# Low halves of three weight blocks made by ScalarE and an adding transfer, in place of a VectorE subtraction

## The chip, the cores and the metric

One program on one core of a Trainium2 chip. The metric is the device time of one execution in microseconds. Before the change the median of three executions is 1394.92 us.

## The reference

Two blocks of a transformer follow each other on 512 tokens of width 1024: a gated MLP layer with a spatial mix, a dilated attention layer, then a second block with two kinds of attention and a feed-forward part. The change lies in that last feed-forward part alone:

```python
D_FF = ((8 * D_MODEL // 3 + 255) // 256) * 256        # 2816
h2 = _modulate(x, ln2_g[l], sh2, sc2)
y = (jax.nn.silu(h2 @ w_gate[l]) * (h2 @ w_up[l])) @ w_down[l]
x = x + g2[:, None, :] * y
```

All arrays are float32.

## The kernel before

**Precision.** Each operand of a matmul is kept as two tiles: a high half, which is the value rounded to float32r by a ScalarE copy, and a low half, the value minus the high half, made by a VectorE subtraction. A product is then three matmuls: high by high, high by low, low by high.

**The feed-forward part.** The 2816 hidden columns are 22 chunks of 128. `FF_GROUPS` cuts them into three groups of 8, 8 and 6 chunks. The first four chunks of group 0 are "whole" (plain matmuls), and the other 18 are "fast" chunks: 4 in group 0, 8 in group 1, 6 in group 2. After each group four "down" chunks multiply by `w_down`.

**A fast chunk.** The gate and up weights of a chunk are cut into four blocks of 128x512 that lie side by side in one raw tile `w_raw` (1 MB, 128x2048). A scheme of Strassen's kind computes the chunk with seven products of 12 matmuls (128x256) each. Their weights are seven blocks: B11, B22 and B21 are blocks of the raw tile as they stand (`PLAIN`), while P1, T3, T2 and T4 are sums, made on VectorE by `two_sums`, `three_sum` and `four_sum`. For each of the seven, `part_round` (ScalarE, L1103) writes the high half into a slot of `w_hi` and `part_rest` (VectorE, L1977) the low half into a slot of `w_lo`.

**Order on TensorE.** For chunk i: product 1 (B11) of i, product 3 (B22) and 4 (T4) of i-1, then product 6 (T2), 5 (P1), 2 (B21), 7 (T3) of i. Each slot of `w_hi` and `w_lo` exists once, so the halves for chunk i+1 are written after the product of chunk i that used the slot.

**Order on ScalarE.** For chunk i: the copy of product 1's result out of PSUM (`half_1`, L1108), B11 of i+1, B22 of i, a silu of i-1, T4 of i, `half_2` (L1113), T2 of i+1, the high half of the gated result of i-1, `half_5`, P1 and B21 of i+1, another silu, `half_3`, T3 of i+1. Product 6 waits for `half_1`, product 7 for `half_2`, product 3 for `half_5`, product 4 for `half_3`. Every engine runs its list in order.

**Raw tiles.** There are two `w_raw` tiles, used in turn. SyncE's queue holds the loads, one for each chunk (`tail_load`, L597). The load for a row waits until the row two before it has been read: for a fast chunk that is VectorE's low half of B22.

GpSimd has nothing to do in this part of the kernel. The profile's line numbers are those of the code before; in the changed kernel L1103 is L1123, L1977 is L1999, and so on.

Of the kernel before, what the change touches and what calls it, by code (L numbers as in the profile page):

```python
# [21 lines left out]
F32 = mybir.dt.float32  # L22
F32R = mybir.dt.float32r
ACT = mybir.ActivationFunctionType
# [73 lines left out]


PRODUCT_AT, PART_AT = product_counts(), part_counts()  # L100

# [48 lines left out]
def program(nc, d):  # L152
# [181 lines left out]
    def sem(name):  # L334
        return nc.alloc_semaphore(name)
# [43 lines left out]
    part_made, part_hi_done, part_lo_done, product_done = sem("part_made"), sem("part_hi_done"), sem("part_lo_done"), sem("product_done")  # L379
    half_1_out, half_2_out, half_3_out, half_5_out = sem("half_1_out"), sem("half_2_out"), sem("half_3_out"), sem("half_5_out")  # L380
    gate_first_done, up_first_done, up_second_done = sem("gate_first_done"), sem("up_first_done"), sem("up_second_done")
    silu_first, silu_second = sem("silu_first"), sem("silu_second")


# [29 lines left out]
    def slot_of(tiles, j):  # L414

        return tiles[j // 4][:, TOK * (j % 4):TOK * (j % 4) + TOK]
# [44 lines left out]
    with block:  # L461
# [3 lines left out]
        def _(sp):  # L465
# [122 lines left out]
            def tail_load(n):  # L588

                used = FF_GROUPS[2][1] * 256 if n >= ROW_OF["whole", W_DOWN[2]] else 2048  # L590
                src = weights[bass.ds(n, 1), :, 0:used].rearrange("a p n -> p (a n)")
                kind, before = ROWS[n - 2]
                if kind == "whole":
                    sp.wait_ge(lo_done, before - 1)
                else:
                    sp.wait_ge(part_lo_done, PART_AT[before, B22])
                sp.dma_start(w_raw[n % 2][:, 0:used], src).then_inc(w_loaded[n % 2], 16)  # L597

            for n in range(W_GU1 + 6, W_END):
# [8 lines left out]
        @block.gpsimd  # L608
        def _(pool):
            def stage(j, par):  # L610

                ge(pool, mix_done, j - 1)
                nc.gpsimd.tensor_tensor(v_stage[par][:, :, :], v[:, :, bass.ds(j * P, P)],
                                        v_stat[:, 5, :].unsqueeze(2).broadcast_to([P, TB, P]), ALU.mult).then_inc(v_staged, 1)

            def sum_squares(k, total, tile):

                for m in range(1, KT - 1):
                    pool.wait_ge(sq_ready, 8 * k + m + 1)
                    if m > 1:  # L620
                        pool.wait_ge(sq_added, 6 * k + m - 1)
                    nc.gpsimd.tensor_tensor(total, tile(0) if m == 1 else total, tile(m), ALU.add).then_inc(sq_added, 1)

            nc.gpsimd.memset(one_row[:, :], 1.0).then_inc(one_ready, 1)
            nc.gpsimd.memset(idle[:, :].bitcast(F32), 0.0).then_inc(idle_ready, 1)
            nc.gpsimd.memset(half_r[:, :].bitcast(F32), 0.0).then_inc(half_zeroed, 1)
            nc.gpsimd.memset(eps_tile[:, :], EPS)
            nc.gpsimd.memset(ones_r[:, :].bitcast(F32), 1.0).then_inc(ones_ready, 1)
            pool.wait_ge(half_zeroed, 1)
            pool.wait_ge(ones_ready, 1)  # L630
            for e in range(2):
                if e:
                    pool.wait_ge(half_ready, 1)
                part = slice(64 * e, 64 * e + 64)
                nc.gpsimd.memset(half_r[part, part].bitcast(F32), 1.0).then_inc(half_ready, 1)
            pool.wait_ge(half_ready, 2)
            pool.wait_ge(v_stat_dve, 3)
            stage(0, 0)
            stage(1, 1)
            with pool.Fori(1, AT // 2) as i:  # L640
                for par in range(2):
                    stage(2 * i + par, par)

            sum_squares(1, sq_sum[:, :], lambda m: sq_a[m % 2][:, :])

            def quarters(m):

                pool.wait_ge(exp_done, 4 * m + 4)
                ge(pool, spread_done, m)
                stats = row_stat[:, 0, :, :].rearrange("p k n -> p (k n)").unsqueeze(1).broadcast_to([P, 4, 16])  # L650
                nc.gpsimd.tensor_tensor(row_apart[:, :, :], stats, own_quarter.unsqueeze(2).broadcast_to([P, 4, 16]), ALU.mult).then_inc(apart_done, 1)

            pool.wait_ge(blocks_loaded, 16)
            for m in range(QH):
                quarters(m)
            pool.wait_ge(pv_done, 4 * QH)
            nc.gpsimd.memset(wf_hi[:, :, :].bitcast(F32), 0.0).then_inc(wf_zeroed, 1)
            nc.gpsimd.memset(wf_lo[:, :, :].bitcast(F32), 0.0).then_inc(wf_zeroed, 1)
            sum_squares(2, sq_sum[:, :], lambda m: sq[m % 2][:, :])
            sum_squares(3, sq_sum[:, :], lambda m: sq[m % 2][:, :])  # L660


        @block.scalar
        def _(act):
# [427 lines left out]
            def part_round(i, j):  # L1092

                group, f, n = FAST[i]
                if j in PLAIN:
                    act.wait_ge(w_loaded[n % 2], 16 * (n // 2))
                else:
                    act.wait_ge(part_made, 3 * i + {P1: 1, T3: 1, T2: 2, T4: 3}[j])
                if i == FAST_OF[group][0]:
                    act.wait_ge(mm_done, 2 * W_DOWN[group] - (2 if j < 4 else 0))  # L1100
                else:
                    act.wait_ge(product_done, PRODUCT_AT[i - 1, USED_BY[j]])
                nc.scalar.activation(slot_of(w_hi, j), part_full(i, j), ACT.Copy).then_inc(part_hi_done, 1)  # L1103

            def half_1_copy(i):
                act.wait_ge(product_done, PRODUCT_AT[i, 1])
# [79 lines left out]
        def _(dve):  # L1186
# [764 lines left out]
            def two_sums(i):  # L1951

                n = FAST[i][2]
                dve.wait_ge(w_loaded[n % 2], 16 * (n // 2))
                if i > 0:
                    dve.wait_ge(part_lo_done, PART_AT[i - 1, T3])
                pairs = w_raw[n % 2][:, 0:3 * TOK].rearrange("p (b n) -> p b n", b=3)
                nc.vector.tensor_tensor(part_sums[:, :, :], pairs[:, 0:2, :], pairs[:, 1:3, :], ALU.add).then_inc(part_made, 1)

            def three_sum(i):  # L1960

                dve.wait_ge(part_made, 3 * i + 1)
                if i > 0:
                    dve.wait_ge(part_lo_done, PART_AT[i - 1, T2])
                nc.vector.tensor_tensor(part_three[:, :], part_sums[:, 0, :], block_of(i, 2), ALU.add).then_inc(part_made, 1)

            def four_sum(i):

                dve.wait_ge(part_made, 3 * i + 2)
                if i > 0:  # L1970
                    dve.wait_ge(part_lo_done, PART_AT[i - 1, T4])
                nc.vector.tensor_tensor(part_four[:, :], part_three[:, :], block_of(i, 3), ALU.add).then_inc(part_made, 1)

            def part_rest(i, j):
# [47 lines left out]
            two_sums(0)  # L2022
            three_sum(0)
            four_sum(0)
            for j in (B11, T2, P1, B21):
                part_rest(0, j)
            whole_gate_up(3)
            part_rest(0, T3)
# [1 line left out]
            for group, (first, count, whole) in enumerate(FF_GROUPS):  # L2030
                chunks = FAST_OF[group]
                for i in chunks:
                    if i - 1 in chunks:
                        up_second(i - 1)
                    if i + 1 in chunks:
                        two_sums(i + 1)
                        part_rest(i + 1, B11)
                        three_sum(i + 1)
                    if i - 1 in chunks:
                        up_first(i - 1)  # L2040
                    part_rest(i, B22)
                    part_rest(i, T4)
                    if i - 1 in chunks:
                        gate_up(i - 1)
                    if i + 1 in chunks:
                        four_sum(i + 1)
                        part_rest(i + 1, T2)
                    if i - 1 in chunks:
                        gu_rest(gu_index(i - 1), FAST[i - 1][1])
                    if i + 1 in chunks:  # L2050
                        part_rest(i + 1, P1)
                    gate_sum(i)
                    if i + 1 in chunks:
                        part_rest(i + 1, B21)
                        part_rest(i + 1, T3)
                    else:
                        tail_lo(W_DOWN[group], 256 * count)
# [5 lines left out]
                for c in range(4):  # L2063
# [3 lines left out]
                    if c == 3 and group < 2:  # L2067
                        after = FAST_OF[group + 1][0]
                        two_sums(after)
                        three_sum(after)  # L2070
                        four_sum(after)
                        for j in (B11, T2, P1, B21):
                            part_rest(after, j)
                    for half in range(2):
                        update_x(2 * c + half, G[2 * (w % 2) + half][:, :], GATE_2, 2 * w + half + 1, 1)
# [5 lines left out]
        def _(pe):  # L2081
# [573 lines left out]

            def product(i, j, out, h, k, t, start, stop):

                pe.wait_ge(part_lo_done, PART_AT[i, j])
                wh, wl = [slot_of(tiles, j).rearrange("p (k n) -> p k n", k=4) for tiles in (w_hi, w_lo)]
                a_hi, a_lo = quarter(h[0], k, t), quarter(h[1], k, t)  # L2660
                for n in range(4):
# [174 lines left out]
```

## Time and profile before

| | |
|---|---|
| executions | 1391.29, 1394.92, 2676.14 us, median 1394.92 us |
| profiled execution | 1394.26 us, its span 1392.5 us |
| TensorE clock in that span | full (1.0) |
| fast chunks on TensorE | about 1084 to 1356 us, in three stretches, down chunks between them |

Times in the trace are microseconds from the span's start. PE is TensorE, DVE is VectorE, ACT is ScalarE, POOL is GpSimd, SP is SyncE and SPq its DMA queue. A matmul's row is longer than its step, since matmuls overlap: the next starts 0.12 us later (128x256).

### The profile page before, as it was taken

The page shows a single profiled execution, that of the slowest core. Times are in us where ns is not written, and L with a number is a line of the kernel's source. Part 1 is how long each engine was busy: PE and PEld are TensorE (multiplying, and loading weights), DVE is VectorE, ACT ScalarE, POOL GpSimd, SP SyncE. Part 2 cuts the span into 40 slices and gives each one's busy share as a digit, 9 for nine tenths or more (in the row PEclk, how much of TensorE's full clock was granted, in tenths as well). Part 3 has the DMA queues.
Part 4 walks back from the last instruction along what each step waited for, and adds up shares of the span by engine and source line. Part 5 has one row for each costly group of instructions (what it writes and reads, how often), then busy time and mean ns, then how long its engine had stood idle before and what let it go on. Part 6 is the DMA issues. An engine that isn't in the chain of part 4 may idle for free.

```text
span 1392.5 us, 21415 instructions
## 1 busy us (share of the span) xinstructions
PE 1377.1 (99%) x7922; PEld 1180.0 (85%) x7922; DVE 1060.4 (76%) x1782; ACT 719.8 (52%) x1256; POOL 50.9 (4%) x55
## 2 busy tenths in 40 slices
PE   8999999999999999999999999999999999999999
PEld 6998888888888888888888787777688988998997
DVE  6976777777789688888887867787778946974873
ACT  4744322333356656666654656756656633652551
POOL 0001000000100000000002000000030000000000
PEclk9999999999999999999999999999999999999999
DMA  9995444457733212211112241111031231323222
GB/s 379 381 361 190 174 174 172 173 215 279 298 118 106 92 61 65 88 61 60 60 61 91 83 130 60 63 61 61 32 121 61 91 122 61 122 96 118 91 82 101
DMA packets 35350, 181.51 MB, mean 130 GB/s; under 512 B 4153, under 2 KB 4921, under 8 KB 20930
## 3 DMA queue, kind: packets, MB, share of 16 engines
q1 hardware_dynamic: 34050, 177.95, 35.2%
q10 hardware_dynamic: 1216, 2.44, 0.6%
q8 instruction: 52, 0.85, 0.2%
q14 instruction: 32, 0.26, 0.1%
HBM read 177.74 MB, written 2.11 MB: 129 GB/s over the span
## 4 chain that ended last, share of the span: by engine, by line
PE 87%; DVE 8%; ACT 3%; issue 2%; DMA 0%; ACTq 0%; DVEq 0%
PE acc L2083 65%; PE turn L2663 7%; PE ada L2083 3%; PE norm L2083 3%; PE turn L2083 2%; PE acc L2663 2%; PE norm L2663 2%; PE ada L2663 2%; DVE hx L1191 1%; PE turn L2377 1%; PE turn L2520 1%; DVE w_lo L1199 1%; DVE h_lo L1191 1%; ACT w_hi L1072 1%; DVE w_lo L1932 1%
## 5 line engine op out<-in xcount | busy, mean ns | idle before, releaser
L2083 PE MATMUL acc<-h_hi,w_hi 128*128 128x512 f32 x696 | 277.8, 399 | 0.0
L2083 PE MATMUL acc<-h_hi,w_lo 128*128 128x512 f32 x696 | 272.0, 391 | 0.0
L2083 PE MATMUL acc<-h_lo,w_hi 128*128 128x512 f32 x696 | 271.3, 390 | 0.0
L1199 DVE TENSOR_TENSOR w_lo<-w_raw,w_hi 128x2048 fp32r<-128x2048 f32 x60 | 141.1, 2351 | 26.9 <-ACT w_hi L672 26.8
L2083 PEld LDWEIGHTS acc<-h_hi,w_lo 128*128 128x128 f32 x696 | 130.6, 188 | 28.4
L2083 PEld LDWEIGHTS acc<-h_hi,w_hi 128*128 128x128 f32 x696 | 131.0, 188 | 26.9 <-issue 1.2
L2083 PEld LDWEIGHTS acc<-h_lo,w_hi 128*128 128x128 f32 x696 | 131.0, 188 | 25.5
L672 ACT ACTIVATE w_hi<-w_raw 128x2048 fp32r<-128x2048 f32 x61 | 116.3, 1906 | 29.2 <-PE acc L2083 29.1
L1191 DVE SCALAR_TENSOR_TENSOR x<-acc,mods,x 128x512 f32<-128x512 f32 x48 | 38.7, 815 | 69.6 <-PE acc L2083 69.6
L2083 PE MATMUL acc<-wv_hi,h_hi 128*128 128x256 f32 x320 | 90.5, 284 | 0.0
L2083 PE MATMUL acc<-wv_lo,h_hi 128*128 128x256 f32 x320 | 89.1, 279 | 0.0
L2083 PE MATMUL acc<-wv_hi,h_lo 128*128 128x256 f32 x320 | 88.3, 279 | 0.0
L678 ACT ACTIVATE y<-norm,eps_tile 128x512 f32<-128x512 f32 x54 | 37.2, 689 | 78.3 <-PE norm L2083 76.9
L2083 PE MATMUL acc<-gu_hi,w_hi 128*128 128x512 f32 x176 | 68.7, 390 | 0.1
L2083 PE MATMUL acc<-gu_lo,w_hi 128*128 128x512 f32 x176 | 68.5, 389 | 0.0
L2083 PE MATMUL acc<-gu_hi,w_lo 128*128 128x512 f32 x176 | 68.5, 389 | 0.0
L2083 PEld LDWEIGHTS acc<-wv_hi,h_hi 128*128 128x128 f32 x320 | 60.1, 188 | 1.2 <-issue 1.0
L2083 PEld LDWEIGHTS acc<-wv_lo,h_hi 128*128 128x128 f32 x320 | 60.9, 190 | 0.2
L2083 PEld LDWEIGHTS acc<-wv_hi,h_lo 128*128 128x128 f32 x320 | 59.6, 188 | 0.0
L1103 ACT ACTIVATE w_hi<-w_raw 128x512 fp32r<-128x512 f32 x54 | 33.5, 628 | 35.4 <-PE acc L2083 17.9
L1191 DVE SCALAR_TENSOR_TENSOR ada_out<-ada_out,csil 128x1024 f32<-128x1024 f32 x32 | 38.4, 1222 | 16.6 <-DMA ada_out<-in_ada 16.4
L2083 PE MATMUL acc<-y_hi,w_hi 128*128 128x512 f32 x128 | 49.9, 390 | 0.0
(364 smaller groups left out, 3516.4 us busy)
## 6 DMA issues: line engine op xcount, KB each, us to landing
w_raw<-in_weights SPq DMA_DIRECT2D x102, 1024.0 KB, 4.9
ada_v<-in_ada SPq DMA_DIRECT2D x32, 512.0 KB, 6.3
ada_raw<-in_ada SPq DMA_DIRECT2D x32, 512.0 KB, 5.7
ada_out<-in_ada SPq DMA_DIRECT2D x32, 512.0 KB, 6.4
ada_up<-in_ada_first SPq DMA_DIRECT2D x8, 1024.0 KB, 16.7
w_raw<-in_weights SPq DMA_DIRECT2D x4, 768.0 KB, 4.2
x<-in_x SPq DMA_DIRECT2D x2, 1024.0 KB, 5.9
w_first<-in_weights SPq DMA_DIRECT2D x4, 512.0 KB, 13.3
```

The costliest lines, as they stand in the source:

```text
L672: nc.scalar.activation(weights_at(u, par)[0][:, 0:used], w_raw[par][:, 0:used], ACT.Copy).then_inc(hi_done, 1)
L678: nc.scalar.activation(y0[:, :], total, ACT.Ln, scale=1.0 / count, bias=eps_col).then_inc(ln_done, 1)
L1072: nc.scalar.activation(w_hi[par][:, 0:used], w_raw[par][:, 0:used], ACT.Copy).then_inc(hi_done, 1)
L1103: nc.scalar.activation(slot_of(w_hi, j), part_full(i, j), ACT.Copy).then_inc(part_hi_done, 1)
L1191: return nc.vector.scalar_tensor_tensor(out, in0, scalar, in1, op0, op1, **more)
L1199: nc.vector.tensor_tensor(lo[:, 0:used], w_raw[par][:, 0:used], f32(hi[:, 0:used]), ALU.subtract).then_inc(lo_done, 1)
L1932: nc.vector.tensor_tensor(w_lo[par][:, 0:used], w_raw[par][:, 0:used], f32(w_hi[par][:, 0:used]), ALU.subtract).then_inc(lo_done, 1)
L2083: return nc.tensor.matmul(out, lhsT, rhs, start=start, stop=stop)
L2377: turned = nc.tensor.transpose((T0, T1)[c % 2][:, P * b:P * b + P], s_b[tile][:, lo:lo + P], ident)
L2520: turned = nc.tensor.transpose(T0[:, P * b:P * b + P], s_2[n % 3][:, 0, P * b:P * b + P], ident)
L2663: last = nc.tensor.matmul(out, w_part[:, n, :], a_part[:, n, :], start=start and n + m == 0, stop=stop and n + m == 5, skip_group_check=no ...
```

## The change

For B11, B22 and B21 of each fast chunk the subtraction on VectorE is dropped. In its place ScalarE, right behind the high half, writes minus the high half into the slot of `w_lo` (the same copy with a scale of -1), and GpSimd issues a transfer from the raw block onto that slot with an addition (`accum_op`), so that the slot holds raw minus high. TensorE waits for the transfer's semaphore where it waited for VectorE. The load that overwrites a raw tile waits for all three transfers of the chunk and for VectorE's three sums. The other four blocks are as before; counts of VectorE's low halves are now `REST_AT`, those of the minus copies `PLAIN_AT`.

```diff
+REST_AT = {entry: sum(1 for other in PART_AT if other[1] not in PLAIN and PART_AT[other] <= n) for entry, n in PART_AT.items()}
+PLAIN_AT = {entry: sum(1 for other in PART_AT if other[1] in PLAIN and PART_AT[other] <= n) for entry, n in PART_AT.items()}
...
                 if kind == "whole":
                     sp.wait_ge(lo_done, before - 1)
                 else:
-                    sp.wait_ge(part_lo_done, PART_AT[before, B22])
+                    sp.wait_ge(part_made, 3 * before + 3)
+                    for j in PLAIN:
+                        sp.wait_ge(plain_added[j], 16 * before + 16)
                 sp.dma_start(w_raw[n % 2][:, 0:used], src).then_inc(w_loaded[n % 2], 16)
...
+            def add_plain(i, j):
+
+                pool.wait_ge(minus_done, PLAIN_AT[i, j])
+                pool.dma_start(slot_of(w_lo, j).bitcast(F32), part_full(i, j), accum_op=ALU.add).then_inc(plain_added[j], 16)
+
+            for chunks in FAST_OF:
+                add_plain(chunks[0], B11)
+                add_plain(chunks[0], B21)
+                for i in chunks:
+                    if i + 1 in chunks:
+                        add_plain(i + 1, B11)
+                    add_plain(i, B22)
+                    if i + 1 in chunks:
+                        add_plain(i + 1, B21)
...
                 nc.scalar.activation(slot_of(w_hi, j), part_full(i, j), ACT.Copy).then_inc(part_hi_done, 1)
+                if j in PLAIN:
+                    nc.scalar.activation(slot_of(w_lo, j), part_full(i, j), ACT.Copy, scale=-1.0).then_inc(minus_done, 1)
...
-            for j in (B11, T2, P1, B21):
+            for j in (T2, P1):
                 part_rest(0, j)
...
                         two_sums(i + 1)
-                        part_rest(i + 1, B11)
                         three_sum(i + 1)
                     if i - 1 in chunks:
                         up_first(i - 1)
-                    part_rest(i, B22)
                     part_rest(i, T4)
...
                     if i + 1 in chunks:
-                        part_rest(i + 1, B21)
                         part_rest(i + 1, T3)
...
-                pe.wait_ge(part_lo_done, PART_AT[i, j])
+                if j in PLAIN:
+                    pe.wait_ge(plain_added[j], 16 * i + 16)
+                else:
+                    pe.wait_ge(part_lo_done, REST_AT[i, j])
```

The changed order, first on ScalarE, in the steady part of a group. The rows run from one chunk's `half_1` copy on; `w_hi_61` and `w_hi_62` are the two tiles with the slots of high halves, `w_lo_63` and `w_lo_64` those of low halves, `w_raw_52` and `w_raw_53` the two raw tiles. Before:

```order
L1108 ACTIVATE half_243<-turn 128x256 [waits gate_first_done,product_done]
L1103 ACTIVATE w_hi_61<-w_raw_52 128x512 [waits product_done,w_loaded0]
L1103 ACTIVATE w_hi_62<-w_raw_53 128x512 [waits product_done,w_loaded1]
L1131 ACTIVATE silu_g_232<-turn 128x256 [waits product_done]
L1103 ACTIVATE w_hi_62<-part_four 128x512 [waits product_done,part_made]
L1113 ACTIVATE half_245<-turn 128x256 [waits up_first_done,product_done]
L1103 ACTIVATE w_hi_61<-part_three 128x512 [waits product_done,part_made]
L1077 ACTIVATE gu_hi<-gu_234 128x512 [waits gu_done]
```

The same place in the changed kernel:

```order
L1130 ACTIVATE half_243<-turn 128x256 [waits gate_first_done,product_done]
L1123 ACTIVATE w_hi_61<-w_raw_52 128x512 [waits product_done,w_loaded0]
L1125 ACTIVATE w_lo_63<-w_raw_52 128x512
L1123 ACTIVATE w_hi_62<-w_raw_53 128x512 [waits product_done,w_loaded1]
L1125 ACTIVATE w_lo_64<-w_raw_53 128x512
L1153 ACTIVATE silu_g_232<-turn 128x256 [waits product_done]
L1123 ACTIVATE w_hi_62<-part_four 128x512 [waits product_done,part_made]
L1135 ACTIVATE half_245<-turn 128x256 [waits up_first_done,product_done]
L1123 ACTIVATE w_hi_61<-part_three 128x512 [waits product_done,part_made]
L1097 ACTIVATE gu_hi<-gu_234 128x512 [waits gu_done]
```

Two copies stand newly behind B11 and B22, ahead of the silu, T4 and the `half_2` copy (`half_245`); a third stands behind B21 later in the chunk. On SyncE, the loads at the end of group 0 and the start of group 1, where `w_loaded0` and `w_loaded1` are the semaphores of the raw tiles. In the changed kernel:

```order
L602 DMA w_raw_53<-in_weights 128x2048 [waits lo_done]
L602 DMA w_raw_52<-in_weights 128x2048 [waits plain_added5,plain_added3,plain_added0,part_made]
L602 DMA w_raw_53<-in_weights 128x2048 [waits plain_added5,plain_added3,plain_added0,part_made]
```

The loads behind a fast chunk waited for `part_lo_done` before and now wait for the three transfers (`plain_added0`, `3` and `5` are those of B11, B21 and B22) and the sums; those behind a down chunk wait for `lo_done` as before. GpSimd's list, where the fast chunks begin:

```order
L627 TENSOR_TENSOR sq_sum<-sq_sum,sq_93 128x512 [waits sq_added,sq_ready]
L627 TENSOR_TENSOR sq_sum<-sq_sum,sq_94 128x512 [waits sq_added,sq_ready]
L627 TENSOR_TENSOR sq_sum<-sq_sum,sq_93 128x512 [waits sq_added,sq_ready]
L670 DMA w_lo_63<-w_raw_52 128x512 [waits minus_done] x2
L670 DMA w_lo_63<-w_raw_53 128x512 [waits minus_done]
L670 DMA w_lo_64<-w_raw_52 128x512 [waits minus_done]
```

Before, the list ended with the third row. Now the transfers follow: B11 and B21 of the first chunk, B11 of the second, B22 of the first, and so on, 54 in all.

## Rows read from the trace of the kernel before

**Rows 1.** Page: busy time, share of the span, instructions; TensorE's clock.

```profile
PE 1377.1 (99%) x7922; PEld 1180.0 (85%) x7922; DVE 1060.4 (76%) x1782; ACT 719.8 (52%) x1256; POOL 50.9 (4%) x55
PEclk9999999999999999999999999999999999999999
```

**Rows 2.** Windows in group 1: busy us of each engine (instructions), clock, DMA share, GB/s.

```profile
1182.00:1192.00 10.00, 10.00 (x86) 10.00 (x85) 8.95 (x16) 6.73 (x14) 0.00 (x0) 1.00 0.31 105
1202.00:1212.00 10.00, 10.00 (x86) 10.00 (x85) 8.95 (x16) 6.72 (x14) 0.00 (x0) 1.00 0.30 107
```

**Rows 3.** Waits of TensorE from 1030 us on: total us, times, longest.

```profile
PE turn L2663 <- ACT half L1108: 1.9, 3, 1.0
```

**Rows 4.** Timeline of TensorE: first matmul of products 1, 7, 1, 3.

```profile
1187.97 0.28 PE L2663 MATMUL turn<-h_hi,w_hi 128*128 128x256 f32 x1
...
1196.61 0.28 PE L2663 MATMUL turn<-f_hi,w_hi 128*128 128x256 f32 x1
...
1198.05 0.28 PE L2663 MATMUL turn<-h_hi,w_hi 128*128 128x256 f32 x1
...
1199.49 0.28 PE L2663 MATMUL norm<-f_hi,w_hi 128*128 128x256 f32 x1
```

**Rows 5.** Groups by shape from 1050 us on: busy us, mean ns, idle before.

```profile
L1977 DVE TENSOR_TENSOR w_lo<-w_raw,w_hi 128x512 fp32r<-128x512 f32 x54 | 37.2, 688 | 1.6 <-ACT w_hi L1103 0.9
L1103 ACT ACTIVATE w_hi<-w_raw 128x512 fp32r<-128x512 f32 x54 | 33.5, 628 | 35.4 <-PE acc L2083 17.9 <-PE acc L2663 7.2 <-PE norm L2663 6.3
```

**Rows 6.** Timeline of ScalarE, one chunk: start, us, [idle before <- releaser].

```profile
1189.61 0.38 ACT L1108 ACTIVATE half<-turn 128x256 f32<-128x256 f32 x1 [0.54 <-PE turn L2663]
1189.89 0.62 ACT L1103 ACTIVATE w_hi<-w_raw 128x512 fp32r<-128x512 f32 x1
1191.11 0.64 ACT L1103 ACTIVATE w_hi<-w_raw 128x512 fp32r<-128x512 f32 x1 [0.60 <-PE ada L2663]
1192.49 0.38 ACT L1131 ACTIVATE silu_g<-turn 128x256 f32<-128x256 f32 x1 [0.74 <-PE turn L2663]
...
1196.87 0.63 ACT L1103 ACTIVATE w_hi<-w_raw 128x512 fp32r<-128x512 f32 x1 [0.60 <-PE acc L2663]
...
1199.97 0.62 ACT L1103 ACTIVATE w_hi<-w_raw 128x512 fp32r<-128x512 f32 x1
```

**Rows 7.** Timeline of VectorE and SyncE's queue: low halves of B11, B22, the load.

```profile
1191.18 0.69 DVE L1977 TENSOR_TENSOR w_lo<-w_raw,w_hi 128x512 fp32r<-128x512 f32 x1
...
1192.71 0.69 DVE L1977 TENSOR_TENSOR w_lo<-w_raw,w_hi 128x512 fp32r<-128x512 f32 x1
...
1193.43 0.33 SPq L597 DMA_DIRECT2D w_raw<-in_weights  x1
```

**Rows 8.** DMA: issues by tile, median us to landing; single tiles' minimum, median, maximum.

```profile
out<-x SPq DMA_DIRECT2D x8, 256.0 KB, 2.0
v_b<-v_turn SPq DMA_DIRECT2D x16, 32.0 KB, 2.5
...
DMA to landing us min/median/max: 1.8/2.5/4.7
...
DMA to landing us min/median/max: 4.7/4.8/5.1
```

**Rows 9.** Timeline of ScalarE: starts of group 1 and of group 2.

```profile
1171.60 0.38 ACT L1108 ACTIVATE half<-turn 128x256 f32<-128x256 f32 x1 [0.74 <-PE turn L2663]
1171.88 1.14 ACT L1103 ACTIVATE w_hi<-w_raw 128x512 fp32r<-128x512 f32 x2
...
1179.81 0.62 ACT L1103 ACTIVATE w_hi<-w_raw 128x512 fp32r<-128x512 f32 x1
...
1297.12 1.14 ACT L1103 ACTIVATE w_hi<-w_raw 128x512 fp32r<-128x512 f32 x2
...
1305.04 0.62 ACT L1103 ACTIVATE w_hi<-w_raw 128x512 fp32r<-128x512 f32 x1
```

**Rows 10.** Timeline of ScalarE: start of group 0.

```profile
1086.96 1.14 ACT L1103 ACTIVATE w_hi<-w_raw 128x512 fp32r<-128x512 f32 x2
...
1095.34 0.37 ACT L1108 ACTIVATE half<-turn 128x256 f32<-128x256 f32 x1
1096.26 1.15 ACT L1103 ACTIVATE w_hi<-w_raw 128x512 fp32r<-128x512 f32 x2 [0.54 <-DMA w_raw<-in_weights]
```

More of the change, by code:

```diff
@@ L381, in program @@
     gate_first_done, up_first_done, up_second_done = sem("gate_first_done"), sem("up_first_done"), sem("up_second_done")
+    minus_done, plain_added = sem("minus_done"), {j: sem(f"plain_added{j}") for j in PLAIN}
     silu_first, silu_second = sem("silu_first"), sem("silu_second")
@@ L1955, in two_sums @@
                 if i > 0:
-                    dve.wait_ge(part_lo_done, PART_AT[i - 1, T3])
+                    dve.wait_ge(part_lo_done, REST_AT[i - 1, T3])
                 pairs = w_raw[n % 2][:, 0:3 * TOK].rearrange("p (b n) -> p b n", b=3)
@@ L1963, in three_sum @@
                 if i > 0:
-                    dve.wait_ge(part_lo_done, PART_AT[i - 1, T2])
+                    dve.wait_ge(part_lo_done, REST_AT[i - 1, T2])
                 nc.vector.tensor_tensor(part_three[:, :], part_sums[:, 0, :], block_of(i, 2), ALU.add).then_inc(part_made, 1)
@@ L1970, in four_sum @@
                 if i > 0:
-                    dve.wait_ge(part_lo_done, PART_AT[i - 1, T4])
+                    dve.wait_ge(part_lo_done, REST_AT[i - 1, T4])
                 nc.vector.tensor_tensor(part_four[:, :], part_three[:, :], block_of(i, 3), ALU.add).then_inc(part_made, 1)
@@ L2071, in _ @@
                         four_sum(after)
-                        for j in (B11, T2, P1, B21):
+                        for j in (T2, P1):
                             part_rest(after, j)
```

## The prediction

> **What bounds the kernel now.** Start with the page: TensorE is busy 99% of the span at full clock [rows 1], VectorE 76%, ScalarE 52%. A busy share is a mean, so the stage that the change touches is read next, the 18 fast chunks of the feed-forward part (1084 us to 1356 us). In a stretch of it TensorE is busy all the time, VectorE 8.95 of 10 us, ScalarE 6.72, the DMA engines 0.30 to 0.31 [rows 2]. VectorE is the fullest helper, but fullness only matters if TensorE waits for it. The list of TensorE's waits from 1030 us on has one row: 1.9 us, for `half` copies of ScalarE [rows 3]. No wait for a `w_lo` of these chunks is in it. So what VectorE gives up is worth at most about 2 us, and the question is whether the new path is late.
>
> The rhythm: a chunk has seven products. Product 1 of one chunk starts at 1187.97 and of the next at 1198.05 [rows 4], a period of 10.08 us, 1.44 us each.
>
> **The change, part by part.**
>
> VectorE loses three subtractions of 128x512 per chunk, 688 ns each, 54 in all [rows 5]. They lie under TensorE: worth nothing.
>
> ScalarE gains three copies per chunk. The same copy with the other sign is not in the trace; its nearest row is L1103, 628 ns, and two back to back take 1.14 us [rows 5, 6], 0.52 us apart. So 0.53 us each, 1.6 us per chunk, on 6.73 of 10: not a bound. Where do they fall? In [rows 6] the copy of B11 begins at 1189.89, then ScalarE waits for a product until 1191.11 (B22), then again until 1192.49. Both new copies behind these fit into idle time. The one behind B21 (1196.87) pushes a silu by 0.5 us and the next half copy by 0.1 us, both with over 2 us to spare before product 4, at 1200.93. Cost 0. Below 0 it can go by 0.3 us only: before chunk 0 a VectorE backlog is shorter.
>
> GpSimd gains 54 transfers of 256 KB, each adding 128x512 onto SBUF; nothing else is left in its queue then. What they do to TensorE has two sides.
>
> *Directly*: product 1 of the next chunk starts at 1198.05 [rows 4]. Its low half was ready at 1191.9 (copied at 1189.89, subtracted from 1191.18 in 0.69 us [rows 6, 7]). In the new path it is ready at 1189.89 + 1.16 (two copies) + A, where A is the time from a finished minus copy to a landed add. That leaves 7.0 - A. Nothing is lost below 7 us. B22 and B21 have as much.
>
> *Through the raw buffer*: this is the term that counts. There are two `w_raw`. The load for chunk i+2 used to wait for VectorE's subtraction of B22 of chunk i: it begins at 1192.71, the load is issued at 1193.43 [rows 7] and lands 4.8 us later (4.7 to 5.1) [rows 8], at 1198.2, where ScalarE wants it at 1199.97 for B11 [rows 6]. Slack 1.8 us. Now the load waits for the add. The minus copy of B22 ends at about 1192.3 (1191.11 + 1.16), the add lands at 1192.3 + A, the load at 1197.1 + A. It is late once A is over 2.9 us. Behind it SP has only later loads, but ScalarE, in order, holds B11 and B22 of the next chunks, T4, and the `half` copies that TensorE needs. And it feeds itself: a late load makes B11 and B22 late, so their adds, so the load after. That loop takes four copies (2.2 us), A, and the load (4.85 us with its issue): 7.05 + A against the period of 10.08.
>
> What is A? No GpSimd transfer and no add is in this trace. From below: eight stores of 256 KB on SP's queue land in 2.0 us [rows 8]. From above: moves from SBUF to SBUF of only 32 KB on SP's queue, 16 in a row, take 2.5 us and up to 4.7 [rows 8]; with two passes over 256 KB, 6.3 us. (A pass: 107 GB/s at a share of 0.31 is 345 GB/s for all engines, so 256 KB is 0.8 us [rows 2].) My value is 4.0 us: the store's 2.0, 0.8 for reading the second operand, 0.4 for queueing behind the add of B11 issued 1.06 us earlier (a two-pass add fills the engines for 1.6 us), and 0.8, a choice without a row, for GpSimd making the transfer in software; its bounds are 0 and 2.3, what is left to either end.
>
> The load slows too: late loads share the engines with the add of B21, 1.6 us of engine time. Bounds 0 and 1.6; I take 0.5.
>
> The Trainium skill has a price for a GpSimd transfer ("DMA: Bandwidth & Descriptors", Anatomy of one DMA — SWDGE (gpsimd) path): about 2.0 us plus bytes over 436 GB/s, so 2.6 us for 256 KB, with the estimate of 0.8 us for a second operand 3.4. With 2.6 nothing would be late in the steady rhythm. The page fits plain copies, and no run here shows it.
>
> *The sum.* Lateness X of a load, against the time at which ScalarE wants it, starts in a group's second chunk. In group 1 the first half copy is at 1171.60, the two copies begin at 1171.88, and ScalarE wants the third chunk's raw block at 1179.81, right behind a half copy (7.93 us later; 7.92 in group 2, from 1297.12 to 1305.04) [rows 9]. Now: 1171.88 + 2.2 + 4.0 + 4.85 = 1182.9, so X = 3.1. Each further chunk adds 11.55 - 10.08 = 1.5. TensorE loses nothing until X is over the slack: 7.0 - A = 3.0 for B11; and 3.3 for `half_2`, since product 7 starts at 1196.61 [rows 4] and it is copied by 3.3 us after B11's start in the new order (four copies 2.1, silu 0.3, T4 0.5, half copy 0.4). The last gated load of a group of C chunks is used in its chunk C - 2.
> - Group 1, 8 chunks: 3.1 + 5 x 1.5 - 3.0 = 7.6 us.
> - Group 2, 6 chunks, same start: 3.1 + 3 x 1.5 - 3.0 = 4.6 us.
> - Group 0, 4 chunks: two copies from 1086.96, wanted at 1095.6 (after the half copy at 1095.34; already 0.54 us late on the load) [rows 10]: 1086.96 + 11.05 = 1098.0, X = 2.4, plus 1.5 - 3.0 = 0.9 us.
>
> Together 13.1 us. The down chunk behind a group is copied 7 us later in its phase than B11 would be, so its load still has cover. Between groups the down matmuls give everything time to catch up. The profiled execution took 1394.26 us (span 1392.5 and 1.8 around it), 0.7 under the median 1394.92. Sum 1394.3 + 13.1 = 1407.
>
> **The rivals.**
>
> *Hidden anyway.* The add lands in 3 us or less: then X stays near 2.1, under the slack of 3.3, and the time is 1394 (1392 to 1397). For it: the store of the same size in 2.0 us, DMA engines at 0.31. Against it: two operands and a software issue. By the skill's 2.6 us it would be this case.
>
> *The loop is long, over 2% slower.* Place: the third chunk on, in each group. Price by the same sum: at A = 5.0 X starts at 4.1, the step is 2.5, the slack 2.0, and the groups lose 14.6, 9.6 and 3.8, that is 28 us, 1422; at A = 5.7 about 40 us, 1434. It decides from A = 5 on (2% is 28 us). For it: short moves within SBUF took up to 4.7 us here. A way to get there: VectorE, busy 8.95 of 10 us [rows 2], holding up GpSimd by one instruction (0.69 us) per transfer. On that the Trainium skill ("SBUF — State Buffer", Who interferes with whom) says that a `tensor_tensor` has no 2-port mode and takes only the read side, while making descriptors needs the write side; by that rule this way is closed, and it calls the last part inferred.
>
> *VectorE's relief pays.* All waits of TensorE here are 1.9 us, of them perhaps 0.3 from VectorE's backlog: 1392 to 1394. Never over 2%.
>
> *ScalarE becomes the bound.* 8.3 of 10.08 us, no.
>
> **How the numbers follow.** Small loss, 3 to 28 us: 0.40. Hidden: 0.28. Long loop: 0.30. Relief: 0.02. The likeliest is 1407; its own range is 1397 to 1422. The range that leaves out 2 in 10 takes in the hidden case and the long loop up to A = 5.7: 1392 to 1435. Within 2% (what a measurement can tell from no change): small loss and hidden, 0.68, and the rest of relief; slower 0.30; faster 0.02.
>
> **What would show it.** Right: SP's loads in the fast chunks issued over a microsecond later within the period than at 1193.43, ScalarE waiting for `w_raw` at B11 (once, 0.5 us, before), growing from chunk to chunk in a group; from the fifth chunk or so, TensorE idle before product 1 for the add, or before product 7 for `half_2`; the period of late chunks in group 1 near 11.5 us, that of the first near 10.1. The down stages stay as they are. Wrong: landed adds in 3 us and a period of 10.08 throughout; or TensorE waiting already in the first chunks of a group, which would put A at 6 us or more. Most likely to be wrong is A, next the slowing of loads.

## The result, and the profile after

| | before | changed |
|---|---|---|
| executions, median | 1394.79 us | 1425.94 us (1424.72 to 1428.29) |
| ratio | | 1.023, interval 1.0209 to 1.0252 |
| profiled execution, its span | 1392.5 us | 1424.5 us |
| group 0, product 1 of its first chunk to its first down matmul | 41.78 us | 46.33 us |
| group 1, the same | 81.59 us | 97.85 us |
| group 2, the same | 61.19 us | 72.25 us |

The change made the kernel 2.3% slower. One of the four executions before took 2676.14 us and is left out of the ratio. The three groups of fast chunks hold all of it: 4.55 + 16.26 + 11.06 = 31.9 us of the 32.0 by which the span grew.

The page after: busy times; who holds the chain that ended last; GpSimd's queue (packets, MB, share of 16 engines' span); its transfers' landing.

```profile
PE 1386.5 (97%) x7922; PEld 1182.2 (83%) x7922; DVE 1028.9 (72%) x1728; ACT 740.1 (52%) x1310; POOL 97.4 (7%) x109
...
PE 74%; DMA 9%; DVE 8%; ACT 5%; issue 3%; POOL 1%; ACTq 0%; SPq 0%; DVEq 0%
...
q0 software_dynamic: 7776, 14.16, 5.7%
...
w_lo<-w_raw POOLq DMA_DIRECT2D x54, 256.0 KB, 3.8
```

The chain before:

```profile
PE 87%; DVE 8%; ACT 3%; issue 2%; DMA 0%; ACTq 0%; DVEq 0%
```

VectorE gave up 31.5 us of work and ScalarE took 20.3 more, and the chain now runs through transfers for 9% of the span, where it had none. Who waits, in the fast part (total us, times, longest):

```profile
ACT w_hi L1123 <- DMA w_raw<-in_weights: 50.6, 12, 6.3
...
PE acc L2685 <- DMA w_lo<-w_raw: 18.5, 15, 1.9
PE turn L2685 <- ACT half L1135: 3.9, 11, 1.3
PE turn L2685 <- ACT half L1130: 1.4, 3, 0.5
PE ada L2685 <- DMA w_lo<-w_raw: 0.4, 2, 0.2
```

Against [rows 3], three waits of 1.9 us in all, TensorE has two new kinds: product 2 (its bank is `acc`) for the add of B21, in every chunk but each group's first, and product 7 for `half_2` (L1135). The rows add up to 24.2 us and the loss is 31.9, in part because an idle bracket starts at the modelled end of a matmul's row, 0.28 us behind its start, while the next step would follow after 0.12 us [rows 4]; the lengths of the groups are the measure. Behind both stands ScalarE's wait for the raw tile, 50.6 us, which had been 0.5 us, once [rows 10]. The loop that makes it grow is in the chain of work that ended last, here the first load of group 1 and one turn behind it (start, us):

```profile
1183.37 7.57 DMA w_raw<-in_weights
...
1191.50 0.62 ACT w_lo L1125
...
1192.41 0.86 POOL w_lo L670
...
1193.45 3.82 DMA w_lo<-w_raw
...
1197.39 5.75 DMA w_raw<-in_weights
...
1203.17 0.02 ACT w_hi L1123
```

The raw tile has landed, ScalarE copies B11 and minus B11, GpSimd issues B11's add and then B22's, that add lands, the next load is issued, and it lands at 1203.14, 12.2 us after the one before. TensorE is nowhere in this turn. ScalarE's timeline shows all six waits of group 1 (the bracket is the idle time before the copy):

```profile
1190.96 0.63 ACT L1123 ACTIVATE w_hi<-w_raw 128x512 fp32r<-128x512 f32 x1 [6.33 <-DMA w_raw<-in_weights]
1203.17 0.63 ACT L1123 ACTIVATE w_hi<-w_raw 128x512 fp32r<-128x512 f32 x1 [3.65 <-DMA w_raw<-in_weights]
1215.37 0.63 ACT L1123 ACTIVATE w_hi<-w_raw 128x512 fp32r<-128x512 f32 x1 [3.64 <-DMA w_raw<-in_weights]
1228.79 0.63 ACT L1123 ACTIVATE w_hi<-w_raw 128x512 fp32r<-128x512 f32 x1 [4.87 <-DMA w_raw<-in_weights]
1240.72 0.63 ACT L1123 ACTIVATE w_hi<-w_raw 128x512 fp32r<-128x512 f32 x1 [3.37 <-DMA w_raw<-in_weights]
1252.52 0.63 ACT L1123 ACTIVATE w_hi<-w_raw 128x512 fp32r<-128x512 f32 x1 [3.24 <-DMA w_raw<-in_weights]
```

Five steps in 61.56 us, 12.3 us each, where TensorE's work is 10.08.

### The profile page after: what moved, and what is told of

Same layout as the page of the kernel before. It is cut to its first block, busy times and chain, and to the rows that moved or that the text cites. A ratio compares the mean times of both kernels' runs of the same rounds, so it can differ in the third digit from the quotient of the medians.

```text
span 1424.5 us, 21505 instructions
## 1 busy us (share of the span) xinstructions
PE 1386.5 (97%) x7922; PEld 1182.2 (83%) x7922; DVE 1028.9 (72%) x1728; ACT 740.1 (52%) x1310; POOL 97.4 (7%) x109
## 4 chain that ended last, share of the span: by engine, by line
PE 74%; DMA 9%; DVE 8%; ACT 5%; issue 3%; POOL 1%; ACTq 0%; SPq 0%; DVEq 0%
PE acc L2102 63%; DMA w_raw<-in_weights 5%; DMA w_lo<-w_raw 4%; PE ada L2102 3%; PE norm L2102 3%; PE turn L2102 2%; DVE hx L1213 1%; ACT w_lo L1125 1%; PE turn L2396 1%; PE turn L2539 1%; PE turn L2685 1%; DVE w_lo L1221 1%; ACT w_hi L1123 1%; POOL w_lo L670 1%; DVE h_lo L1213 1%
## 5 line engine op out<-in xcount | busy, mean ns | idle before, releaser
L2102 PEld LDWEIGHTS acc<-h_hi,w_hi 128*128 128x128 f32 x696 | 131.0, 188 | 27.1 <-issue 1.2
L1123 ACT ACTIVATE w_hi<-w_raw 128x512 fp32r<-128x512 f32 x54 | 33.7, 623 | 69.9 <-DMA w_raw<-in_weights 50.6
L670 POOL DMA_DIRECT2D w_lo<-w_raw x54 | 46.5, 862 | 300.1 <-ACT w_lo L1125 297.4
L1980 DVE TENSOR_TENSOR part_sums<-w_raw 128x1024 f32<-128x1024 f32 x18 | 22.0, 1224 | 43.2 <-DMA w_raw<-in_weights 42.9
```

The lines of the kernel that those rows point to most:

```text
L670: pool.dma_start(slot_of(w_lo, j).bitcast(F32), part_full(i, j), accum_op=ALU.add).then_inc(plain_added[j], 16)
L2102: return nc.tensor.matmul(out, lhsT, rhs, start=start, stop=stop)
```

## The experiments

Two theories. *Loop*: a load waits for the add of B22, which in ScalarE's and GpSimd's order stands behind B11 of the next chunk, which waits for a load. *Collision*: the add of B21 travels together with a load, both are slow, and product 2 waits for it. They are not exclusive, so the runs also had to share the loss out between them.

| run | median us | ratio to before, interval | loss in groups 0, 1, 2 (us) |
|---|---|---|---|
| changed kernel | 1425.9 | 1.023 (1.0209 to 1.0252) | 4.6, 16.3, 11.1 |
| e1: B22 ahead of B11 | 1394.9 | 1.0011 (1.0001 to 1.0021) | 0.0, 0.6, 2.0 |
| e2: B21 on VectorE | 1411.7 | 1.0129 (1.0108 to 1.0150) | 1.0, 8.4, 7.1 |
| e3: B22 on VectorE | 1394.1 | 1.0003 (0.9993 to 1.0013) | -0.4, 0.0, 0.0 |
| e4: only B22 new | 1396.9 | 1.0023 (1.0012 to 1.0035) | 0.0, 2.4, 1.5 |
| e5: plain copies | 1394.7 | 1.0006 (0.9996 to 1.0016) | -0.3, 1.0, 0.5 |
| e6: half loads | 1407.7 | 1.0094 (1.0075 to 1.0113) | 1.4, 6.5, 5.9 |
| e7: ScalarE copies only | 1393.0 | 0.9992 (0.9982 to 1.0003) | 0.0, 0.0, 0.0 |
| e8: adds aside | 1392.8 | 0.9993 (0.9982 to 1.0003) | 0.0, 0.0, 0.0 |
| e9: B21's traffic, not its wait | 1422.4 | 1.0206 (1.0187 to 1.0225) | 3.1, 14.0, 10.4 |

The ratios compare medians; the losses are those of one profiled execution each. The interval of e9 lies on both sides of 2%.

**e1, B22 ahead of B11.** The same in the table that counts the low halves.

```diff
                     half_1_copy(i)
-                    if i + 1 in chunks:
-                        part_round(i + 1, B11)
                     part_round(i, B22)
+                    if i + 1 in chunks:
+                        part_round(i + 1, B11)
...
+                    add_plain(i, B22)
                     if i + 1 in chunks:
                         add_plain(i + 1, B11)
-                    add_plain(i, B22)
```

> The changed kernel with one swap: ScalarE and GpSimd handle B22 of chunk i ahead of B11 of chunk i+1, so the add that frees a raw tile no longer stands behind a copy that waits for the other raw tile. Loop theory (a late load delays the next add in order): the load is issued near 1196.2 instead of growing later, lands before it is wanted, and the time falls to 1396 to 1401; ScalarE's waits for w_raw fall from 50.6 us to under 10. Collision theory (the add of B21 travels with a load and is late for product 2 whatever the order): TensorE keeps waiting for w_lo in every chunk and the time stays at 1420 to 1426.

Measured 1394.9 us, a little below the expected span. Nothing of the 54 copies and 54 adds is taken away, and the time falls by 31 us, to 1.0 us over the kernel before. The groups still lose 2.6 us together. TensorE's waits in the fast part, and ScalarE at a chunk's start (the first copy is B22's now):

```profile
PE turn L2693 <- DMA w_lo<-w_raw: 1.8, 5, 0.6
PE turn L2693 <- ACT half L1133: 1.4, 3, 0.5
```

```profile
1199.29 0.63 ACT L1126 ACTIVATE w_hi<-w_raw 128x512 fp32r<-128x512 f32 x1 [1.12 <-PE norm L2693]
1199.83 0.62 ACT L1128 ACTIVATE w_lo<-w_raw 128x512 fp32r<-128x512 f32 x1
1200.35 0.62 ACT L1126 ACTIVATE w_hi<-w_raw 128x512 fp32r<-128x512 f32 x1
```

ScalarE waits for TensorE's product 3 again and then finds the raw tile of B11 there. B22's add no longer depends on a load, so lateness has no way round. B21's add still meets a load: it is issued at 1196.39, 1.6 us behind the load of 1194.8, and lands in 4.6 us, in time for product 2; the loads land in 4.8 to 5.2 us in the steady part. The swap thus did two things: it cut the loop, and it moved the load from 0.7 us ahead of B21's add to 1.6 us ahead of it. Which of the two counts, e2 has to tell.

**e2, B21 on VectorE; e3, B22 on VectorE; e4, only B22 on the new path.** One edit in three settings:

```diff
+ADDED = (B11, B22)          # e3: (B11, B21); e4: (B22,)
...
-                if j in PLAIN:
+                if j in ADDED:
                     nc.scalar.activation(slot_of(w_lo, j), part_full(i, j), ACT.Copy, scale=-1.0).then_inc(minus_done, 1)
```

> The changed kernel, with B21 alone back on VectorE. Loop theory: the loop stays (copies and issue 2.5 us, add 3.8, load 4.9, together 11.3 against 10.08), minus the collision; a loss of about 12 us against before, 1405 to 1410. Collision theory: product 2 no longer waits for an add, so 1394 to 1398.

> The changed kernel, with B22 alone back on VectorE; B11 and B21 still added by transfers. Loop theory: no load waits for a fresh add, so 1394 to 1398, loads issued within 1 us of where they were before. Collision theory: B21's add is still there; if it is the add as such that is late for product 2, 1405 or more.

> Only B22 on the new path. Loop theory: a loop of 1.7 (copies) + 0.3 + 3.7 (a single add) + 0.1 + 4.9 = 10.7 us, 0.6 over the period; with 3 us of slack about 4 us lost, 1396 to 1402. Collision theory: no add gates product 2: 1395, as before.

e2 at 1411.7 us is 2 us over its span: the loop alone, without a collision, costs 16.5 us in the groups. Its loads in the loop of group 1 land in 4.9 us in the median (4.7 to 5.9), its turns there are 11.1 to 12.3 us, 11.5 on average, and TensorE now waits at the place that the slack sum names second:

```profile
PE turn L2694 <- ACT half L1139: 10.9, 11, 1.8
PE turn L2694 <- ACT half L1134: 1.4, 3, 0.5
```

e3 and e4 came out as the loop theory said. Taking B22 off the new path takes away the whole loss, though 36 adds remain. With B22 alone on it the loop is short (one copy and one add fewer) and the loss is 3 us (3.9 in the groups). Its turns are 10.2 to 11.8 us; the longest follows a load that took 6.4 us with no add under way, to which the last section comes back.

**e5, the transfers as plain copies.**

```diff
-                pool.dma_start(slot_of(w_lo, j).bitcast(F32), part_full(i, j), accum_op=ALU.add).then_inc(plain_added[j], 16)
+                pool.dma_start(slot_of(w_lo, j).bitcast(F32), part_full(i, j)).then_inc(plain_added[j], 16)
```

> The changed kernel with the 54 transfers as plain copies, without the addition (the low halves of three blocks are then the raw values, so the output means nothing). If the second operand is what makes A long: landing falls from 3.8 to about 3.2 us, engine time per transfer from 1.3 to 0.8 us, the loop from 12.2 to about 11.2 us, the time to 1405 to 1415. If the price is GpSimd's issue and the collision as such: landing stays above 3.6 and the time at 1420 to 1427.

1394.7 us, far below both expectations: the addition costs more than I gave it. Of e5: GpSimd's group (mean 540 ns), its queue, and landing of the transfers (minimum, median, maximum):

```profile
L673 POOL DMA_DIRECT2D w_lo<-w_raw x54 | 29.1, 540 | 287.2 <-ACT w_lo L1128 287.2
...
q0 software_dynamic: 4320, 14.16, 2.6%
...
DMA to landing us min/median/max: 2.3/2.3/6.2
```

The output of e5 means nothing, only its time counts. GpSimd's group in the changed kernel:

```profile
L670 POOL DMA_DIRECT2D w_lo<-w_raw x54 | 46.5, 862 | 300.1 <-ACT w_lo L1125 297.4 <-issue 2.7
```

Adding takes GpSimd 0.86 us per transfer and not 0.54, 144 packets and not 80, and 1.5 us of all engines (5.7% of 1424.5 over 54) and not 0.67; it lands in 3.3 to 3.8 us and not 2.3. With plain copies the loads are issued 10.1 us apart (1195.22 and 1205.34), and the loop just fits the period.

**e6, half loads.**

```diff
-                used = FF_GROUPS[2][1] * 256 if n >= ROW_OF["whole", W_DOWN[2]] else 2048
+                used = 1024 if ROWS[n][0] == "fast" else FF_GROUPS[2][1] * 256 if n >= ROW_OF["whole", W_DOWN[2]] else 2048
```

> The changed kernel with the loads of fast chunks cut to the first 1024 of 2048 columns (B22 and B21 then come from stale data). Loop theory: the load's part of the loop falls from 5.8 to about 3.5 to 4.2 us, the loop to 10 to 10.6, the time to 1394 to 1402. If TensorE waits for adds for a reason apart from the loads, 1415 or more.

1407.7 us, between the two spans. The six halved loads of group 1 took 4.2 us in the median (3.7 to 5.0), with adds beside them all the same, and five turns from 1184.82 to 1238.65 are 10.8 us each, still over 10.08. The direction and size fit the loop: 1.5 us off a turn and 2.6 off the first load (5.0 in place of 7.6) took 18 of the 31.9 us in the groups.

**e7, ScalarE's copies alone; e8, the traffic alone.** In e7 the kernel before also writes minus the high half into the slot, and VectorE overwrites it after waiting for it. In e8 GpSimd issues 54 adds that nobody waits for.

```diff
# e7, added to the kernel before
+                if j in PLAIN:
+                    nc.scalar.activation(slot_of(w_lo, j), part_full(i, j), ACT.Copy, scale=-1.0).then_inc(minus_done, 1)
# e8, added to the kernel before
+                pool.wait_ge(part_hi_done, PART_AT[i, j])
+                dst = x_rstd[:, :] if j == B22 else consts[:, K_DIST:K_DIST + TOK]
+                pool.dma_start(dst, h_hi[:, j, :].bitcast(F32), accum_op=ALU.add).then_inc(aside[j], 16)
```

> The kernel before with ScalarE's 54 minus copies added into the slots of w_lo, which VectorE then overwrites with its subtraction as before; no transfers. The sum of the prediction has them at no cost: 1393 to 1397. If ScalarE's extra 1.6 us per chunk had a share in the loss, 1400 or more.

> The kernel before with 54 adding transfers of 256 KB from GpSimd beside it, paced by the same high halves, from a tile that rests to two tiles that nobody reads; nothing waits for them but the next one. Loop theory: traffic alone costs nothing, loads land in 5 to 6.5 us inside or near their slack of 1.8 us, 1393 to 1398. If sharing engines is the cause without the wait: 1405 or more.

Neither costs anything. So ScalarE's 1.6 us per chunk and the engines' load are not causes by themselves. But e8 shows what sharing does to landing: the adds to `x_rstd` (in B22's place), most of them 0.5 us behind another add and close to a load, and then the loads of the fast part:

```profile
DMA to landing us min/median/max: 4.3/7.1/8.7
...
DMA to landing us min/median/max: 4.3/5.1/7.4
```

An add that lands in 3.3 us where it is the only one (e4) takes 7.1 us there in the median, and a load of 4.8 us up to 7.4. ScalarE waited 9.9 us for such loads, and none of it reached TensorE. These adds do not read a raw tile, so it is not the shared tile that makes them slow.

**e9, B21's traffic without its wait.** B21's minus copy and add go to a spare tile at their old times, loads wait for them as in the changed kernel, and VectorE makes B21's low half. The loads wait for that half too, and ScalarE waits for the last add to the spare tile before it writes there again.

```diff
+                to = slot_of(w_lo, j) if j in ADDED else consts[:, K_DIST:K_DIST + TOK]
...
-                nc.scalar.activation(slot_of(w_lo, j), part_full(i, j), ACT.Copy, scale=-1.0).then_inc(minus_done, 1)
+                nc.scalar.activation(slot_of(w_lo, j) if j in ADDED else consts[:, K_DIST:K_DIST + TOK], part_full(i, j), ACT.Copy, scale=-1.0).then_inc(minus_done, 1)
```

> The changed kernel's traffic with one wait less: B21's minus copy and its adding transfer go to a tile that nobody reads, at the same times as in the changed kernel, and VectorE makes B21's low half as before, so product 2 does not wait for a transfer. Loads still wait for all three adds. If the rest of the loss (the 14 us between 1412 with B21 wholly on VectorE and 1426) comes from loads slowed by sharing engines with that add: 1420 to 1427. If it comes from product 2 waiting for the add: 1410 to 1415.

1422.4 us. TensorE's waits, and the landing of loads in group 1:

```profile
PE turn L2695 <- ACT half L1140: 19.6, 12, 2.8
PE turn L2695 <- ACT half L1135: 1.4, 3, 0.5
...
DMA to landing us min/median/max: 5.3/5.9/7.3
```

With product 2's wait gone, product 7's wait for `half_2` takes its place, and in sum little changes: up to the start of each group's last chunk the groups lose 27.0 us here, against 27.1 in the changed kernel. Only the last chunks differ: they lose 0.3, 0.2 and 0.1 us here, and 1.8, 1.9 and 1.0 in the changed kernel. There B21's add is issued 0.65 us behind the first load for the down chunks, lands 6.7 us later, and product 2 waits (group 1 of the changed kernel):

```profile
1258.96 0.33 SPq L602 DMA_DIRECT2D w_raw<-in_weights  x1
1259.61 0.86 POOL L670 DMA_DIRECT2D w_lo<-w_raw  x1 [3.75 <-ACT w_lo L1125]
...
1266.48 0.36 PE L2685 MATMUL acc<-h_hi,w_hi 128*128 128x256 f32 x1 [1.50 <-DMA w_lo<-w_raw]
```

Elsewhere product 2's wait is covered: without it the loop makes product 7 wait instead. That shares out the 15.4 us between e2 and the changed kernel in the groups: 11.0 us are the loop made longer by B21's minus copy and add (in group 1, 2.0 us at the first load and 3.6 in the five turns; copy and traffic were not taken apart), 4.4 us are product 2's wait, 4.2 of them in the last chunks. By the medians the shares are 10.6 and 3.6 us. One thing blurs them: in e9's profiled execution TensorE's granted clock was 0.5 (1.2 and not 2.4 GHz) twice for 3.4 us, from 1217.76 and from 1344.06, the first time after a stretch in which TensorE was busy for 1.3 of 3 us; the changed kernel's has no such stretch before its end. Neither lies in a last chunk; what they cost was not measured.

No version beats the kernel before: TensorE waited 1.9 us in this part [rows 3], and e3, e5, e7 and e8 can't be told from it.

## Why the prediction was right or wrong

1407 was forecast, 1426 measured: inside the range of 1392 to 1435, but outside the 1397 to 1422 of the case held likeliest. The loss was 31 us and not 13, and the case over 2%, given 0.30, is what happened. The mechanism was right; the sum took too little for the loads and nothing for the last chunk.

- **VectorE's relief is worth nothing, ScalarE's copies cost nothing**: right (e7; e3 at 1.0003). The relief shows as 0.4 us in group 0 of e3, where the prediction allowed 0.3. (A relief that is "never over 2%" cannot carry the 0.02 that it gave to "faster".)
- **Through the raw buffer**: right in mechanism. The loop is in the chain as described. e1 breaks it and gives back all but 2.6 us, and e2, with the loop and no collision, keeps 16.5.
- **A = 4.0 us**: right. B22's minus copy ended at 1205.36, its add landed at 1209.46: 4.1 us. Its parts were not: the addition costs 1.0 us where an add is alone and 1.5 behind another one (e4, e5), not 0.8 and 0.4 on top, and a plain transfer from GpSimd lands in 2.3 us, only 0.3 over SP's store, where I had given GpSimd 0.8; the 0.3 us from the copy's end to GpSimd's issue I had left out. The errors cancelled, which was luck. "It decides from A = 5 on" was wrong: it happened at 4.1. (The upper bound of GpSimd's own term was misread too: 2.3 us is what lies above the whole 4.0, the term alone could have gone to 3.1.)
- **"The load slows too ... I take 0.5"**: the step that failed, and twice. In the turns of group 1 loads took 5.4 to 6.6 us, 5.8 on average, and so 0.95 more than 4.85 and not 0.5. The first load of group 1 took 7.6 us, 2.7 more, and the sum's start had no slowing at all for it. B21's add is issued just ahead of it, in the short first chunk:

```profile
1182.87 0.86 POOL L670 DMA_DIRECT2D w_lo<-w_raw  x1 [2.94 <-ACT w_lo L1125]
...
1183.37 0.33 SPq L602 DMA_DIRECT2D w_raw<-in_weights  x1
```

  That is not all of the reason: a fetch of instructions fell into that load as well (last section), and in group 0, where the add was issued 0.14 us ahead, the load took 5.8 us. The load was also issued 0.5 us after the add that it waited for had landed, elsewhere 0.12; why stays open. So ScalarE's first wait was 6.3 us and not 3.1.
- **The slack of 3.0 us**: right, with 3.1 measured (below), though it was product 2 and product 7 that used it up, not product 1.
- **B21's add at 4 us ("B22 and B21 have as much")**: the second step that failed. In the changed kernel B21's adds took 5.9 to 8.7 us beside a load. Within a group that is covered by the loop, but behind the last turn nothing covers it: 4.7 us in the three last chunks, for which the sum had nothing.

The sum again for group 1, with what was measured: ScalarE's first wait, plus what five turns take beyond five periods (50.4 us), less what TensorE has lost at the start of the last chunk, gives the slack.

| us | first wait | five turns | lost at the last chunk's start | slack | lost in the last chunk |
|---|---|---|---|---|---|
| forecast | 3.1 | 7.5 | 7.6 | 3.0 | 0 |
| changed kernel | 6.3 | 11.2 | 14.4 | 3.1 | 1.9 |
| e2 | 4.1 | 7.3 | 8.3 | 3.1 | 0.1 |
| e4 | 3.2 | 2.5 | 2.1 | 3.6 | 0.2 |
| e6 | 3.8 | 3.4 | 4.1 | 3.1 | 2.4 |
| e9 | 6.1 | 10.9 | 13.9 | 3.1 | 0.2 |

The slack comes out the same, 3.1 us, wherever ScalarE makes all its copies ahead of `half_2`; in e4, where B11 has no minus copy and `half_2` comes one copy sooner, it is 0.5 us more. Of the 8.7 us that the forecast missed in group 1, 3.2 are the first load, 3.7 the turns, 1.9 the last chunk, less 0.1 for the slack. Where no collision is, in e2, the turn of 11.5 us is the forecast one, and the sum's 0.9, 7.6 and 4.6 us stand against 1.0, 8.4 and 7.1.

- **The signs**: SP's loads later in the period and ScalarE's wait at B11, as named. Wrong were three. TensorE lost time from each group's second chunk, not from the fifth; the sum itself, with 3.1 us of lateness against 3.0 of slack, had put the start there. It was product 2, not 1, that waited for an add. And a wait so early was to mean that A is 6 us or more, while A was 4.1: the first load was late for other reasons.
- **Hidden anyway**: fell, though e5 shows how near it was: with transfers that land 1.5 us sooner it would have been the result. The estimate of 2.6 us from the page's figures (the Trainium skill, "DMA: Bandwidth & Descriptors", Anatomy of one DMA) is close to the plain copies of e5, at 2.3; it does not hold for adds, at 3.3 alone and 3.8 behind another.
- **GpSimd held up by VectorE**: did not happen. Issues took 0.86 us each (the first of all 1.01) with VectorE busy most of the time, in line with the page "SBUF — State Buffer" of the Trainium skill (Who interferes with whom).

## What to carry to other kernels

When work moves onto a buffer's last reader, follow the loop from a buffer's release round to its next release through the queues' order, and add it up against the period. A loop that passes through another buffer's load in an in-order queue feeds itself, and swapping two entries may cut it: here that was worth 31 us. Price transfers in the company they will have in that loop, not alone, above all in a group's first, shorter round, and look at the last round by itself, since no later turn covers a wait there.

## What the runs showed of the hardware

- A transfer from GpSimd that adds 128x512 float32 within SBUF takes 0.86 us to issue and 3.3 us to land alone, with 144 packets and about 1.5 us of the 16 engines; a plain one 0.54 us, 2.3 us, 80 packets and about 0.67 us.
- An add and a 1 MB load that overlap can slow each other by more than their engine time (1.5 us, and 3.1 for the load: a share of 0.31 over 10.08 us [rows 2]): the add from 3.3 up to 8.7 us, the load from 4.8 up to 7.7 us. When they meet matters: load 1.6 us ahead of the add, 4.9 and 4.6 us (e1); 0.7 us ahead, 5.8 and 6.4; add 0.13 us ahead of the load, 7.7 and 8.7 in group 2, but 0.14 us ahead only 5.8 and 7.3 in group 0 (all in the changed kernel). So the order of issue is not the whole of it. What arbitrates between them was not tried.
- Loads that met a fetch of instructions took longer. In e2 and e4, where no add starts in the first 3.5 us of a load, 12 of the 1 MB loads in the fast part took 5.4 to 6.5 us. Into the first 3.5 us of each of these fell a transfer of 16 KB of the queue that the profile's page calls "q8 instruction", 0.9 to 2.2 us long by the packets in the trace, and into none of the others, which took 5.1 us at most. One such transfer fell into the first load of group 1 of the changed kernel (2.1 us long) and one into the load of 1222.15, which took 6.6 us. No run here took these fetches away, so their share in the loss is not known.
